# The latent delta rule's query decay: its bound, its exponential and its score product are taken out of the four key rounds and put into the levels of the inverse

## What is computed

```python
def gated_delta_chunked(q, k, v, beta, g, s0):
    ...
    g = jnp.cumsum(g, axis=-1)
    decay = jnp.exp(jnp.where(lower, g[..., :, None] - g[..., None, :], -jnp.inf))
    kb = k * beta[..., None]
    a = jnp.where(strict, jnp.einsum("bhnid,bhnjd->bhnij", kb, k) * decay, 0.0)
    t_inv = lax.linalg.triangular_solve(a + eye, ...)
    u = t_inv @ (v * beta[..., None])
    w = t_inv @ (kb * jnp.exp(g)[..., None])
    attn = jnp.einsum("bhnid,bhnjd->bhnij", q, k) * decay
    ...
    def step(s, inp):
        v_new = u_i - jnp.einsum("bhcd,bhde->bhce", w_i, s)
        o_i = jnp.einsum("bhcd,bhde->bhce", qg_i, s) + jnp.einsum("bhij,bhje->bhie", attn_i, v_new)
        ...
```

## Time and profile before

| | us |
|---|---|
| median of 3 runs (1247.64 to 1248.5) | 1247.96 |
| the profiled execution | 1248.19 |
| its span | 1246.3 |
| key rounds, first line 1318 to the end of the last line 1301 | 808.22 to 831.45 |
| levels of the inverse, first line 945 to the last line 965 | 839.25 to 893.2 |

### The profile page before, as it was taken

How to read it: one execution, slowest core, us unless ns; L and a number is a source line. 1 busy time by engine, 2 the same in 40 slices (tenths; PEclk the granted TensorE clock), 3 DMA queues, 4 the chain that set the end, 5 groups by cost and what they waited for, 6 DMA issues and landing times.

```text
span 1246.3 us, 21010 instructions
## 1 busy us (share of the span) xinstructions
PE 1213.4 (97%) x8476; PEld 1106.8 (89%) x8476; DVE 900.3 (72%) x1285; ACT 667.7 (54%) x1055; POOL 65.6 (5%) x62
## 2 busy tenths in 40 slices
PE   8999999999999999999999999979999999999997
PEld 7989999998999899999999889869988998888886
DVE  6788777777879287767757776786567876766666
ACT  6574544445666376545364665645646555544434
POOL 0330000000034030000000000200000000000000
PEclk9999999999999999999999999989999999999999
DMA  9627677666763453465646765512225566655560
GB/s 325 201 83 239 195 244 238 234 220 197 246 206 103 135 169 122 150 188 164 205 154 236 226 182 167 160 54 65 96 68 179 193 206 204 232 180 174 188 202 34
DMA packets 161102, 220.24 MB, mean 177 GB/s; under 512 B 5776, under 2 KB 135662, under 8 KB 160878
## 3 DMA queue, kind: packets, MB, share of 16 engines
q1 hardware_dynamic: 159282, 215.50, 53.2%
q10 hardware_dynamic: 1724, 3.39, 0.7%
HBM read 217.04 MB, written 1.05 MB: 175 GB/s over the span
## 4 chain that ended last, share of the span: by engine, by line
PE 81%; DVE 8%; ACT 5%; issue 1%; DMA 1%; DVEq 1%; ACTq 1%; SPq 1%
PE bank L568 19%; PE bank L570 18%; PE bank L569 18%; PE bank L617 9%; PE bank L619 5%; DVE w_lo L559 3%; PE bank L682 2%; PE bank L957 2%; PE bank L945 1%; DMA w_raw<-in_w_in 1%; ACT w_hi L550 1%; PE bank L965 1%; PE bank L1543 1%; DMA arena<-arena 1%; PE bank L974 1%
## 5 line engine op out<-in xcount | busy, mean ns | idle before, releaser
L559 DVE TENSOR_TENSOR w_lo<-w_raw,w_hi 128x1024 fp32r<-128x1024 f32 (+1 forms) x350 | 419.5, 1239 | 65.7 <-ACT w_hi L550 55.4
L550 ACT ACTIVATE w_hi<-w_raw 128x1024 fp32r<-128x1024 f32 (+1 forms) x350 | 350.1, 1041 | 112.7 <-PE bank L570 54.0
L568 PE MATMUL bank<-act_parts,w_hi 128*128 128x256 f32 x1232 | 355.9, 289 | 5.4 <-DVE w_lo L559 2.5
L569 PE MATMUL bank<-act_parts,w_hi 128*128 128x256 f32 x1232 | 349.3, 284 | 0.0
L570 PE MATMUL bank<-act_parts,w_lo 128*128 128x256 f32 x1232 | 349.2, 283 | 0.0
L568 PEld LDWEIGHTS bank<-act_parts,w_hi 128*128 128x128 f32 x1232 | 236.9, 192 | 14.0 <-issue 10.1
L569 PEld LDWEIGHTS bank<-act_parts,w_hi 128*128 128x128 f32 x1232 | 237.1, 192 | 1.3 <-issue 0.7
L570 PEld LDWEIGHTS bank<-act_parts,w_lo 128*128 128x128 f32 x1232 | 236.9, 192 | 0.0
L617 PE MATMUL bank<-act_parts,w_hi 128*128 128x512 f32 x512 | 181.3, 398 | 0.2 <-DVE act_parts L2370 0.2
L568 PE MATMUL bank<-w_hi,side_hi 128*128 128x512 f32 (+1 forms) x384 | 146.5, 381 | 0.0
L570 PE MATMUL bank<-w_hi,side_lo 128*128 128x512 f32 (+1 forms) x384 | 144.7, 377 | 0.0
(11 more groups left out here) (364 smaller groups left out, 1619.3 us busy)
## 6 DMA issues: line engine op xcount, KB each, us to landing
w_raw<-in_w_in SPq DMA_DIRECT2D x39, 1024.0 KB, 5.8
w_raw<-in_w_up SPq DMA_DIRECT2D x32, 1024.0 KB, 6.2
w_raw<-in_w_down SPq DMA_DIRECT2D x32, 1024.0 KB, 4.9
w_raw<-in_w_ffn_in SPq DMA_DIRECT2D x22, 1024.0 KB, 5.2
w_raw<-in_w_gate SPq DMA_DIRECT2D x20, 1024.0 KB, 5.3
w_raw<-in_w_mod SPq DMA_DIRECT2D x32, 512.0 KB, 4.1
w_raw<-in_w_ffn_out SPq DMA_DIRECT2D x11, 1024.0 KB, 5.4
w_raw<-in_w_out SPq DMA_DIRECT2D x8, 1024.0 KB, 5.5
```

The lines of the kernel that those rows point to most:

```text
L550: nc.scalar.activation(whi[:, slot, 0:n], raw[:, st.slot(name), n * half:n * (half + 1)], ACT.Copy).then_inc(hi_ready, 1)
L559: nc.vector.tensor_tensor(wlo[:, slot, 0:n], raw[:, st.slot(name), n * half:n * (half + 1)], whi[:, slot, 0:n].bitcast(F32), ALU.subtract) ...
L568: nc.tensor.matmul(o, ahi, bhi, start=start, stop=False, skip_group_check=True)
L569: nc.tensor.matmul(o, ahi, blo, start=False, stop=False, skip_group_check=True)
```

## The change

The bound of the queries' tile and its exponential leave the four key rounds. The subtraction now writes the difference straight into `g_dec`, where it stays. In level lv of 1 to 4, behind the product of line 1369, DVE bounds group `BY_CHUNK[lv - 1]`, and ACT takes its exponential behind the keys and values of that level; for it ACT waits for that bound (`lat_du`). The `qk` products of chunk 0 and chunk 1 stand at the head of levels 3 and 5 on PE, and the score products of both directions of a chunk stand on DVE in the same level, behind its masked z. ACT's wait for all four score products in level 1, which kept the tiles that it overwrites, becomes a wait for the fourth product of keys. Line numbers of the changed kernel are a few higher.

```diff
+QK_LEVELS = (3, 5)
...
@@ pe_delta, key rounds
-                if lat and d == 0:
-                    b = C(f"qk{g}")
-                    ...
@@ pe_delta, levels
             for lv in range(1, LEVELS):
+                if lat and lv in QK_LEVELS:
+                    n = QK_LEVELS.index(lv)
+                    b = C(f"qk{n}")
+                    pe.wait_ge(S("lat_qn"), 2)
+                    for hh in range(DN_H):
+                        mm = nc.tensor.matmul(ps[b][:, P * hh:P * (hh + 1)], k_n[:, hh, P * n:P * (n + 1)],
+                                              q_n[:, hh, P * n:P * (n + 1)], start=True, stop=True)
+                    F(mm, b)
@@ act_delta, key rounds
-                    act.wait_ge(S("lat_du"), i + 1)
-                    nc.scalar.activation(g_dec[:, g, :], g_dec[:, g, :], ACT.Exp).then_inc(S("lat_eu"), 1)
@@ act_delta, levels
                 if lat and lv <= 4:
                     if lv == 1:
                         act.wait_ge(*told("bcol", 1))
-                        act.wait_ge(S("lat_attn"), 4)
+                        act.wait_ge(*told("A", 4))
                     values_rated(lv - 1)
+                    g = BY_CHUNK[lv - 1]
+                    act.wait_ge(S("lat_du"), lv)
+                    nc.scalar.activation(g_dec[:, g, :], g_dec[:, g, :], ACT.Exp).then_inc(S("lat_eu"), 1)
@@ dve_delta, key rounds
-                free(nc.vector.tensor_tensor(h4(scr[0]), h4(ps[b][:, :]), per_head(gcol[:, g, :]), ALU.subtract), b)
+                free(nc.vector.tensor_tensor(h4(g_dec[:, g, :]), h4(ps[b][:, :]), per_head(gcol[:, g, :]), ALU.subtract), b)
                 dve.drain()
-                nc.vector.tensor_tensor(h4(scr[1 + i % 2]), h4(scr[0]), all_heads(col(f"lo{d}", 0, P)), ALU.max).then_inc(
+                nc.vector.tensor_tensor(h4(scr[1 + i % 2]), h4(g_dec[:, g, :]), all_heads(col(f"lo{d}", 0, P)), ALU.max).then_inc(
                     S("dn_dl"), 1)
-                nc.vector.tensor_tensor(h4(g_dec[:, g, :]), h4(scr[0]), all_heads(col(f"up{d}", 0, P)),
-                                        ALU.min).then_inc(S("lat_du"), 1)
                 key_products(i, g)
-                b = W(f"qk{n}")
-                dve.wait_ge(S("lat_eu"), i + 1)
-                ins = nc.vector.tensor_tensor(g_dec[:, g, :], ps[b][:, :], g_dec[:, g, :], ALU.mult)
-                ...
@@ dve_delta, levels
+            def queries_decayed(n):
+                b = W(f"qk{n}")
+                dve.wait_ge(S("lat_eu"), 2 * n + 2)
+                for d in range(2):
+                    ins = nc.vector.tensor_tensor(g_dec[:, 2 * d + n, :], ps[b][:, :], g_dec[:, 2 * d + n, :], ALU.mult)
+                    ins.then_inc(S("lat_attn"), 1)
+                free(dve.drain(), b)
...
+                if lat and lv in QK_LEVELS:
+                    queries_decayed(QK_LEVELS.index(lv))
                 fill(f"z{lv}")
...
                     nc.vector.tensor_tensor(h4(g_q[:, g, :]), tok(q_n, g % 2), h4(g_q[:, g, :]), ALU.mult).then_inc(
                         S("lat_qg"), 1)
+                    d, g = lv - 1 & 1, BY_CHUNK[lv - 1]
+                    nc.vector.tensor_tensor(h4(g_dec[:, g, :]), h4(g_dec[:, g, :]), all_heads(col(f"up{d}", 0, P)),
+                                            ALU.min).then_inc(S("lat_du"), 1)
                 fill(f"x{lv}")
```

More of the change, by code:

```diff
@@ L1317, in dve_delta @@
                 dve.wait_ge(S("lat_egrow"), i + 1)
-                free(nc.vector.tensor_tensor(h4(scr[0]), h4(ps[b][:, :]), per_head(gcol[:, g, :]), ALU.subtract), b)
+                free(nc.vector.tensor_tensor(h4(g_dec[:, g, :]), h4(ps[b][:, :]), per_head(gcol[:, g, :]), ALU.subtract), b)
                 dve.drain()
-                nc.vector.tensor_tensor(h4(scr[1 + i % 2]), h4(scr[0]), all_heads(col(f"lo{d}", 0, P)), ALU.max).then_inc(
+                nc.vector.tensor_tensor(h4(scr[1 + i % 2]), h4(g_dec[:, g, :]), all_heads(col(f"lo{d}", 0, P)), ALU.max).then_inc(
                     S("dn_dl"), 1)
-                nc.vector.tensor_tensor(h4(g_dec[:, g, :]), h4(scr[0]), all_heads(col(f"up{d}", 0, P)),
-                                        ALU.min).then_inc(S("lat_du"), 1)
                 key_products(i, g)
-                b = W(f"qk{n}")
-                dve.wait_ge(S("lat_eu"), i + 1)
-                ins = nc.vector.tensor_tensor(g_dec[:, g, :], ps[b][:, :], g_dec[:, g, :], ALU.mult)
-                if d == 1:
-                    free(ins, b)
-                dve.drain().then_inc(S("lat_attn"), 1)
                 fill(f"T{i}")
```

## The result

The changed kernel takes 1259.14 us (median of 4 runs, 1257.8 to 1259.57) against 1247.97 us: a ratio of 1.0087, 95% interval 1.007 to 1.0105. That is 11.2 us more, where 6.0 were forecast and 1257.8 was the end of the range. The direction was right, the size was not.

A forecast was written before the change was run, and what follows sets the result against it. PE was taken as busiest, waiting for the DVE-ACT chain in the key rounds and DVE's masked z in the levels. Profiled 1248.19 - 3.40 + 9.32 = 1254.11 us, 1253.88 on the median, stated as 1254.0; range 1250.2 to 1257.8.

The forecast's parts named there:

- What bounds each place: Key rounds: the chain between DVE and ACT; levels: PE, waiting for DVE's masked z, with no slack in DVE.
- Key rounds, 3.40 us less: Key rounds: score products leave the chain, saving 2 x 0.88 + 2 x 0.82 us; removing bound and exponential gives nothing.
- The clock behind the key rounds, no change: Behind the key rounds: PE's idle stretch shrinks from 6.33 to 4.55 us, with the same slow stretch as before.
- The bound and the wait in series, 4 x 2.33 us: Levels 1 to 4: ACT waits for DVE's bound, DVE for ACT's weight half; each masked z 2.33 us later, 9.32 in all.
- 1.11 us: Levels: estimate for the new DVE bound by the DRAIN page, 0.69 + 0.42 us; set aside for the trace's 0.61.
- Score products and `qk`, 0: Levels 3 and 5: the moved products fit into idle time of DVE and PE, costing nothing.
- my bounds of 0 to 1.6: Levels 3 and 5: range in us for the cost of both `qk` together if these levels had no slack.
- the clock falls in a new gap: Rival, chance 0.10: PE's clock falls to 0.50 in the gap before `xz`, up to 3.5 us longer, giving 1257.5 us.
- The range: Whole kernel: 1250.2 us (clock up, 2 us of delay taken up by slack) to 1257.8, leaving out about 0.17.
- both unknown costs in full: Levels 3 and 5 without slack: `qk` up to 1.6 us and score products up to 2.8 us; named for the range's end.

The follow-up runs named there:

- the products alone: Kernel before with only the `qk` and score products moved to levels 3 and 5, bound and exponential staying in the key rounds: 1245.38 us, ratio 0.9983.
- the exponential behind: Changed kernel with ACT's queries' exponential moved behind its halves of weight tiles in levels 1 to 4: 1247.48 us, ratio 0.9996.
- the bound early: Changed kernel with DVE's queries' bound moved up directly behind its masked z in levels 1 to 4: 1245.76 us, ratio 0.9986.
- the wait alone: Kernel before, nothing moved, with ACT waiting for DVE's product for queries ahead of its weight halves in levels 1 to 4: 1254.62 us, ratio 1.0055.
- PE kept busy: Unread products ahead of `xz`, levels 2 to 5: changed kernel 1254.75 us (12, 9, 9, 5) or 1254.47 (4 each); kernel before plus ACT's wait 1252.91 (4 each).
- the version with level 1 set free: Changed kernel with ACT's exponential behind the weight halves in level 1 alone, levels 2 to 4 waiting as they did: 1253.14 us, ratio 1.0044.

## Why the prediction was wrong

Step by step, in its own order:

- **What bounds each place** was right. DVE was the last to arrive in levels 2 to 5, and each delay reached PE without loss. PE's idle time ahead of level 5's `xz` was 1.42 us and not the 2.3 to 3 that I announced, because `qk` fills 0.8 us of it; the distance grew by the forecast 2.33 all the same.
- **Key rounds, 3.40 us less**: 3.18 measured, 3.5 with the products alone. The round of 3.56 us came out as written. In round 3 of the changed kernel DVE waits 0.54 us instead of 0.19 ahead of its subtraction, for nothing that the profile names; the versions with the exponential behind and with the bound early show the same 0.54 us, the kernel that keeps bound and exponential there does not. Why is open.
- **The clock behind the key rounds, no change**: the idle stretch was 4.92 us (I had 4.55), the clock fell as assumed, and the slow stretch was shorter, 6.8 us instead of 10.2. The way from the rounds to level 1 came out 0.58 us shorter, but this is no fixed gain: other versions with the same 6.8 us needed 10.45 to 11.14 us there, against 11.15 before.
- **The bound and the wait in series, 4 x 2.33 us**: confirmed in size (2.34 and 2.33 where the clock stayed up) and in cause, since taking the wait away returns it and the wait alone in the kernel before makes its share of it. Beside this term the prediction set a page against its own row: The Trainium skill, VectorE: DVE Perf Modes, The DRAIN you can't avoid. That paragraph also says that a next instruction that is not held back starts earlier, which the prediction left out. The changed kernel has these starts 0.61 us apart (843.81 and 844.42), so 1.11 us is not the price of this pair.
- **Score products and `qk`, 0**: right as long as PE and DVE idle there, which is what the stall itself provides. Without the stall `qk` costs 0.77 us in level 5, inside my bounds of 0 to 1.6.
- **The clock in the levels, put at nothing in the sum and kept as the rival "the clock falls in a new gap": this is the step that failed.** I gave it 0.10, priced it as a single fall of up to 3.5 us, and took as evidence the one fall that the profile of before had: 3 us into a stretch with no matmul at all. From that I read that a gap shorter than 3 us between dense work is safe. It is not. The clock fell two or three times in each profile of the changed kernel, and with the wait alone it fell behind a gap of 2.0 us. One fall cost 1.4 to 2.8 us, so the price of one was not too low; that they repeat was missing. All levels together they cost 4.3 us. With the smaller misses (0.2 in the key rounds, -0.6 behind them, 0.1 in level 6) 1254.0 + 4.3 becomes 1258.0, of the 1259.1 measured. The remaining 1.1 us is the open remainder named above.
- **The range** ended at 1257.8, named as one fall or both unknown costs in full. The second is 1254.0 + 1.6 + 2.8 = 1258.4, so the end was below its own working. Even that would not have held the measured time.

That a slow clock was the excess in the levels is shown, not argued: the granted clock reads 0.50 where the matmuls are slow, and with PE kept busy the excess vanished from the changed kernel and from the one with the wait alone. What decides whether a gap of about 2 us lets the clock fall is open. The gap of 2.30 us had a fall in one profile of the changed kernel and none in the other, and one of 2.24 us had a fall there and none in the version with level 1 set free, so a sum from one profile can price such a fall but not place it.

## What to carry to other kernels

Before you let an engine wait for another, list what stands behind the wait in its queue, and look whether the engine that it waits for needs any of it next: two engines with in-order queues then work in series, and the price is the whole chain from signal to signal, not the instruction you moved. Put the consumer of a late value behind what others need, or its producer into an idle stretch, and the same work is free. In a stage like this one, count every new gap of 2 us or more on TensorE as a possible fall of its clock, several times over if the gap repeats, and put the case into the range with its full weight.

## What the runs showed of the hardware that I had not expected

TensorE's granted clock went from 1.00 to 0.50 in or just behind idle stretches of 2.0 to 2.9 us between dense work, and stayed there for 3.4 to 6.8 us. In the profiles this happened at seven of the ten such gaps; behind the gaps between dense work in the levels that were shorter, up to 1.77 us, it did not happen. In four of the seven the clock fell only after PE was busy again, in three of these more than a microsecond after. The same 16 matmuls took 3.78 us instead of 2.05. 0.9 us of unread products in front of each such gap kept the clock up in the one profile of each of the two kernels in which it was tried, with gaps of up to 2.01 us still left.
